# A hybrid encoder layer on one core: retention's products with the state split into high and low parts, divisions moved to ScalarE

## The reference, cut to what matters

```python
def sink_attention(q, k, v, valid, sinks):
    ...
    m = jnp.maximum(jnp.max(s, axis=-1, keepdims=True), sink)
    p = jnp.exp(s - m)
    w = p / (jnp.sum(p, axis=-1, keepdims=True) + jnp.exp(sink - m))
    return jnp.einsum('...hgqk,...khd->...qhgd', w.astype(v.dtype), v)

def retention_block(state, q, k, v, log_g):
    ...
    s = jnp.einsum('blhd,bmhd->bhlm', q, k) * decay
    intra = jnp.einsum('bhlm,bmhe->blhe', s, v)
    cross = jnp.einsum('blhd,bhde->blhe', q, state) * jnp.exp(log_g[None, :] * (n[:, None] + 1.0))[None, :, :, None]
    ...
    new_state = (jnp.exp(log_g * float(L))[None, :, None, None] * state
                 + jnp.einsum('blhd,blhe,lh->bhde', k, v, k_dec))
    return new_state, intra + cross
```

## Time and profile before

| | us |
|---|---|
| median of three runs (lowest, highest) | 969.23 (968.95, 969.66) |
| the profiled execution, its own time | 969.13 |
| span of that profile, first to last instruction | 967.30 |

### The profile page before, as it was taken

The page is one execution under the profiler, slowest core; times in us unless marked ns, Lnnn a source line. Parts: engine busy times, 40 slices in busy tenths (PEclk is TensorE's granted clock), DMA queues, the critical chain, the costliest instruction groups (busy, mean ns, idle before and its releaser), DMA issues.

```text
span 967.3 us, 19316 instructions
## 1 busy us (share of the span) xinstructions
PE 957.4 (99%) x7231; PEld 940.6 (97%) x7231; DVE 632.6 (65%) x1271; ACT 488.4 (50%) x955; POOL 158.4 (16%) x222
## 2 busy tenths in 40 slices
PE   8999999999999999999999999999999999999998
PEld 8999999999999999999999999999999999999998
DVE  5554776768666634345449677788778977755772
ACT  5333544445244522222546467776767767644352
POOL 2123212212110000000001202223222322230000
PEclk9999999999999999999999999999999999999999
DMA  8534221221222222344702537758876887776321
GB/s 218 151 114 136 65 70 50 71 77 50 78 71 64 79 77 81 95 121 142 218 23 61 220 113 166 174 130 176 185 171 136 177 184 161 169 225 198 88 56 44
DMA packets 178026, 118.12 MB, mean 122 GB/s; under 512 B 16224, under 2 KB 167168, under 8 KB 177680
## 3 DMA queue, kind: packets, MB, share of 16 engines
q1 hardware_dynamic: 160192, 79.19, 28.9%
q0 software_dynamic: 15856, 36.07, 17.6%
q10 hardware_dynamic: 1888, 1.64, 0.6%
HBM read 86.79 MB, written 10.75 MB: 101 GB/s over the span
## 4 chain that ended last, share of the span: by engine, by line
PE 94%; DVE 3%; issue 1%; ACT 1%; DMA 0%; POOL 0%; SPq 0%; DVEq 0%; POOLq 0%; ACTq 0%
PE acc L799 35%; PE acc L1081 13%; PE acc L1082 13%; PE acc L1083 13%; PE small L1081 4%; PE small L1083 4%; PE small L1082 4%; PE small L945 1%; PE small L962 1%; PE small L998 1%; PE acc L907 1%; PE small L1259 1%; DVE wlo L1872 0%; PE small L954 0%; DMA x_row<-in_x_sample 0%
## 5 line engine op out<-in xcount | busy, mean ns | idle before, releaser
L799 PE MATMUL acc<-xh,whi 128*128 128x288 f32 x720 | 158.7, 301 | 2.9 <-DVE wlo L1872 2.5
L799 PE MATMUL acc<-xl,whi 128*128 128x288 f32 x720 | 153.4, 294 | 0.0
L799 PE MATMUL acc<-xh,wlo 128*128 128x288 f32 x720 | 153.4, 294 | 0.0
L1291 ACT ACTIVATE whi<-raw 128x1024 fp32r<-128x1024 f32 (+1 forms) x60 | 60.1, 1001 | 130.0 <-PE acc L799 128.4
L799 PEld LDWEIGHTS acc<-xh,whi 128*128 128x128 f32 x720 | 113.9, 188 | 9.1 <-issue 7.7
L799 PEld LDWEIGHTS acc<-xh,wlo 128*128 128x128 f32 x720 | 115.0, 188 | 0.0
L799 PEld LDWEIGHTS acc<-xl,whi 128*128 128x128 f32 x720 | 114.9, 188 | 0.0
L1081 PE MATMUL acc<-yh,whi 128*128 128x288 f32 x380 | 112.9, 297 | 0.0
L1083 PE MATMUL acc<-yh,wlo 128*128 128x288 f32 x380 | 112.0, 295 | 0.0
L2800 POOL DMA_DIRECT2D wlo<-raw x80 | 69.0, 863 | 240.6 <-ACT wlo L1540 235.5
L1872 DVE TENSOR_TENSOR wlo<-raw,whi 128x1024 fp32r<-128x1024 f32 (+1 forms) x62 | 71.7, 1156 | 44.1 <-ACT whi L1291 43.4
(11 more groups left out here) (391 smaller groups left out, 2497.3 us busy)
## 6 DMA issues: line engine op xcount, KB each, us to landing
raw<-in_w_in SPq DMA_DIRECT2D x91, 256.0 KB, 3.2
wlo<-raw POOLq DMA_DIRECT2D x56, 256.0 KB, 4.1
raw<-in_w_ffn_gate SPq DMA_DIRECT2D x44, 256.0 KB, 3.4
raw<-in_w_ffn_up SPq DMA_DIRECT2D x44, 256.0 KB, 4.0
raw<-in_w_ffn_down SPq DMA_DIRECT2D x40, 192.0 KB, 3.1
res<-x_scratch POOLq DMA_DIRECT2D x16, 288.0 KB, 4.3
wlo<-raw POOLq DMA_DIRECT2D x24, 192.0 KB, 3.8
raw<-in_w_branch_ret SPq DMA_DIRECT2D x16, 256.0 KB, 3.0
```

Of the source, the lines that this page charges most:

```text
L799: ins = nc.tensor.matmul(acc[:, a, hf, 0:HALF], w[:, s, at:at + P], x(k)[:, hf * HALF:(hf + 1) * HALF], start=first and n == 0 and m == 0, ...
L1291: nc.scalar.activation(whi[:, s, 0:n], raw[:, s, 0:n], ACT.Copy).then_inc(hi_ready, 1)
```

## The change

- The product with the state is split like the others: `dec` has three parts (`q_dec`, `s_dec`, `k_dec`), `dec_hi` and `dec_lo` with it. ACT copies the state to `state_hi` (128x256) in step B of tiles 0 to 3, DVE makes `state_lo` in step L of tiles 1 to 4, and PE's plain f32 product becomes three `fp32r` ones. `state_hi` lies in the memory of `k_row`, so its first copy waits for the transfers from there.
- The probabilities are multiplied by the reciprocal on ACT, in four instructions of one head each with the reciprocal as a per-partition scale, at the same place N.
- The copies for the last block go ahead of the sigmoid of unit 5 of head 3.

```diff
-        q_dec = place("q_dec", [P, 2, P])
-        dec_hi = place("dec_hi", [P, 2, P], F32R)
-        dec = place("dec", [P, 2, P], at=cursor[0])
-        dec_lo = place("dec_lo", [P, 2, P], F32R)
-        s_dec, k_dec = dec[:, 0, :], dec[:, 1, :]
+        dec_hi = place("dec_hi", [P, 3, P], F32R)
+        dec = place("dec", [P, 3, P], at=cursor[0])
+        dec_lo = place("dec_lo", [P, 3, P], F32R)
+        q_dec, s_dec, k_dec = (dec[:, n, :] for n in range(3))
...
@@ PE, retention
                 elif piece == "B":
-                    pe.wait_ge(ret_low, n + 1)
-                    pe.wait_ge(ret_qd, n + 1 + CREDIT)
+                    pe.wait_ge(ret_low, (2 * RT - 1) * r + 2 * c + 1)
...
-                    split_product(ret_o, 0, v, True, c == 0)
+                    split_product(ret_o, 1, v, True, c == 0)
                     if c > 0:
-                        nc.tensor.matmul(ret_o, q_dec[:, c % 2, :], (state_s if c == RT - 1 else state_p)[:, :],
-                                         start=False, stop=True)
-                    split_product(ret_dl, 1, v, True, True).then_inc(ret_B, 1)
+                        split_product(ret_o, 0, (state_hi[:, :], state_lo[:, :]), False, True)
+                    split_product(ret_dl, 2, v, True, True).then_inc(ret_B, 1)
@@ ACT, attention
+                elif piece == "N":
+                    act.wait_ge(att_den, n + 1)
+                    for j in range(GROUP):
+                        ins = nc.scalar.activation(prob[0:nq, j, k0:k1], prob[0:nq, j, k0:k1], ACT.Copy,
+                                                   scale=den[0:nq, j:j + 1])
+                    ins.then_inc(att_prob, 1)
@@ ACT, retention
+                elif piece == "B" and c < RT - 1:
+                    act.wait_ge(ret_state, n + 1 + CREDIT)
+                    if c == 0 and r == 0:
+                        act.wait_ge(out_done, 16 * 6)
+                    if c == RT - 2:
+                        act.wait_ge(state_in_s, 16 * (r + 1))
+                    nc.scalar.activation(state_hi[:, :], (state_s if c == RT - 2 else state_p)[:, :], ACT.Copy
+                                         ).then_inc(ret_high, 1)
@@ ACT, heads
                     if t == 5:
                         v_high(1, h)
+                        if h == RH - 1:
+                            act.wait_ge(att_staged, RH + 1)
+                            act.wait_ge(ckt_ready, 1)
+                            act.wait_ge(cache_in, 32)
+                            nc.scalar.activation(k_st[:, 0:P], ckt[:, :], ACT.Copy)
+                            nc.scalar.activation(v_st[:, 0, :], cva[:, :], ACT.Copy).then_inc(cache_staged, 1)
                     head_job(t, h)
                     pieces(2 * t + 1, b, r, h)
...
-            act.wait_ge(att_staged, RH + 1)
-            act.wait_ge(ckt_ready, 1)
-            act.wait_ge(cache_in, 32)
-            nc.scalar.activation(k_st[:, 0:P], ckt[:, :], ACT.Copy)
-            nc.scalar.activation(v_st[:, 0, :], cva[:, :], ACT.Copy).then_inc(cache_staged, 1)
@@ DVE, attention
                     nc.vector.reciprocal(den[0:nq, :], den[0:nq, :]).then_inc(att_den, 1)
-                    dve.wait_ge(att_den, n + 1)
-                    width = k1 - k0
-                    shares = den[0:nq, :].rearrange("p (j o) -> p j o", o=1).to_broadcast([nq, GROUP, width])
-                    nc.vector.tensor_tensor(prob[0:nq, :, k0:k1], prob[0:nq, :, k0:k1], shares, ALU.mult
-                                            ).then_inc(att_prob, 1)
@@ DVE, retention
                 if piece == "A":
-                    dve.wait_ge(ret_B, n + 1 + CREDIT - earlier_use(c))
+                    dve.wait_ge(ret_B, n + CREDIT)
...
                 elif piece == "L":
-                    dve.wait_ge(ret_high, n + 1)
+                    if c > 0:
+                        dve.wait_ge(ret_high, (2 * RT - 1) * r + 2 * c)
+                        nc.vector.tensor_tensor(state_lo[:, :], (state_s if c == RT - 1 else state_p)[:, :],
+                                                state_hi[:, :].bitcast(F32), ALU.subtract).then_inc(ret_low, 1)
+                    dve.wait_ge(ret_high, (2 * RT - 1) * r + 2 * c + 1)
                     nc.vector.tensor_tensor(dec_lo[:, :, :], dec[:, :, :], dec_hi[:, :, :].bitcast(F32), ALU.subtract
                                             ).then_inc(ret_low, 1)
```

More of the change, by code:

```diff
@@ L428, in encoder_layer @@
         ck_row = place("ck_row", [P, P])
+        state_hi = place("state_hi", [P, RV], F32R, at=cursor[0])
         k_row = place("k_row", [P, 2, P])
@@ L459, in encoder_layer @@
         grstd = place("grstd", [P, 1])
+        state_lo = place("state_lo", [P, RV], F32R)
         split_at = (nc.sbuf_usable_end - 3 * slab) // 32 * 32
@@ L571, in encoder_layer @@
         x_saved_v = sem("x_saved_v")
-        ret_kst, ret_qd, ret_A, ret_sd, ret_kd = (
-            sem("ret_kst"), sem("ret_qd"), sem("ret_A"), sem("ret_sd"), sem("ret_kd"))
+        ret_kst, ret_A, ret_sd, ret_kd = (
+            sem("ret_kst"), sem("ret_A"), sem("ret_sd"), sem("ret_kd"))
         ret_B, ret_state, ret_mom, ret_grstd, ret_norm, ret_C, ret_gated = (
@@ L985, in ret_piece @@
                     pe.wait_ge(v_rows, 2 * r + 2)
-                    if c == RT - 1:
-                        pe.wait_ge(state_in_s, 16 * (r + 1))
                     v = (v_hi[slot][:, c, :], v_lo[:, slot, c, :])
@@ L2015, in ret_piece @@
                 if piece == "A":
-                    dve.wait_ge(ret_B, n + 1 + CREDIT - earlier_use(c))
+                    dve.wait_ge(ret_B, n + CREDIT)
                     q = qr[:, span(slot, 1), c * P:(c + 1) * P].rearrange("p a n -> p (a n)")
-                    nc.vector.tensor_tensor(q_dec[:, c % 2, :], q, tab[:, span(T_QD + P * r, P)], ALU.mult).then_inc(ret_qd, 1)
+                    nc.vector.tensor_tensor(q_dec, q, tab[:, span(T_QD + P * r, P)], ALU.mult)
                     dve.wait_ge(ret_A, n + 1 + CREDIT)
@@ L2651, in settled @@
                 pool.sem_inc(passed, 1)
-            for s_ in (ret_kst, ret_qd, ret_A, ret_sd, ret_kd, ret_B, ret_state, ret_grstd, ret_norm, ret_C,
+            for s_ in (ret_kst, ret_A, ret_sd, ret_kd, ret_B, ret_state, ret_grstd, ret_norm, ret_C,
                        ret_gated):
```

## The result

The changed kernel takes 974.30 us (median of five runs, 973.05 to 975.10) against 969.23 for the kernel before: a ratio of 1.0048 with an interval of 1.0037 to 1.0059. It is slower by 5.1 us; the forecast was 972.5, and its range ended at 974.2. The profiled execution took 975.10 us, the longest of the five, with a span of 973.3.

What follows compares the result with a forecast made beforehand. The prediction took TensorE (PE) as the bound, busy 957.4 of 967.3 us. Its terms, -1.3 - 0.35 + 1.38 + 3 x (-0.45 + 1.20 + 0.45) = +3.3 us on 969.23, gave 972.5, range 969.6 to 974.2.

Steps and rivals of the forecast that it cites:

- products with the state: Tiles 1 to 4 of four heads: three split products take PE 0.08 us less than one f32 product, -1.3 us.
- the last block's copies: Before the last block's scores: copies made before the sigmoid end PE's wait for `v_st`, -0.35 us.
- stall before unit 2: Heads 1 to 3: PE's 0.78 us wait for `wlo` shrinks as DVE's rotation starts earlier, -0.45 us a head.
- `o_norm` of tile 2: Place 5, heads 1 to 3: POOL's rotation delays `dec_lo`, so PE's transposes of `o_norm` start late, +1.20 us a head.
- divisions at place 7: Heads 1 to 3: ACT's four divisions end after PE wants the probabilities for its transposes, +0.45 us a head.
- divisions of the last block: Place 7 of the last block: ACT runs the gate's sigmoid first, so PE gets the divisions late, +1.38 us.
- Who goes next, POOL or `dec_lo`: Place 5, after `state_lo`: POOL's waiting rotation goes first and `dec_lo` follows it, making PE wait +1.20 us a head.
- DVE keeps its turn: Rival, 0.22: at place 5 `dec_lo` follows `state_lo` and POOL waits for both; +1.1 us, 970.3.
- Cheap divisions: Rival, 0.08: ACT's four divisions run at the plain copy's pace, 1.33 us; 968.7 to 970.9.
- More is late: Rival, 0.10: before unit 2 the rotation's `tb` isn't earlier, because ACT's swaps slip further; +1.35 us on top, 973.9.
- It does what it seems to be for: Rival, 0.08: PE gets its probabilities in time everywhere, with fast divisions and POOL last; faster, 966.2 us.

Runs made afterwards that it cites:

- split_only: Changed kernel with only the products with the state split; divisions stay on VectorE, the last block's copies behind the sigmoid: 972.41 us, 1.0037.
- pool_later: Changed kernel, with GpSimd's rotation of unit 2 in heads 1 to 3 also waiting for tile 2's low part: 970.55 us, 1.0012.
- swaps_first: The kernel called reordered, with ACT's two rotation swaps of unit 0 also put ahead of its `split_hi`: 965.67 us, 0.9962.
- reordered: Changed kernel: `state_lo` of tiles 2 to 4 a place earlier, N first at place 7, last block's divisions ahead of the sigmoid: 966.40 us, 0.9978.

## Why the prediction was right and wrong

The direction and the mechanism of each part were right; the sum lacked one term that lay outside the edited third. By starts of PE's rows, after against before, each against the row ahead of it:

| term of the sum | forecast | measured |
|---|---|---|
| products with the state, 16 | -1.3 | -1.3 (16 x 0.08) |
| the last block's copies | -0.35 | -0.42 |
| stall before unit 2, three heads | -1.35 | -0.39, -0.41, -0.40: -1.20 |
| `o_norm` of tile 2, three heads | +3.60 | +1.21, +1.57, +1.35: +4.13 |
| divisions at place 7, three heads | +1.35 | +0.38, +0.38, +0.38: +1.14 |
| the row behind each of these six stalls | none | 6 x 0.06: +0.34 |
| divisions of the last block | +1.38 | +1.28 |
| to the merge | +3.3 | +4.0 |
| behind the merge | 0 | +1.95 in the profiled execution, none in some others |

- **Products**: step B of tile 1 went from 1.13 to 232.69 - 231.64 = 1.05 us, as forecast. PE's busy time doesn't show it: in the stretch it is 314.95 before and 314.99 after. Where PE stops, the tail of its last matmuls counts as busy; at 247.99 the row's idle time is 1.19, and the start moved by 1.35. Seven new stalls hide the 1.3 us.
- **Who goes next, POOL or `dec_lo`**: the step that decided the sign was right. It rested on one hand-over in head 0; split_only gives 1.21 in each head against the forecast 1.20, and pool_later takes it away. The page "SBUF — State Buffer" of the Trainium skill, section "Who interferes with whom", has the exclusion but not who follows: here the one that waits goes between two queued instructions of the other, in each of the three heads, here and in split_only. The rival "DVE keeps its turn" falls.
- **`o_norm`, mis-sized**: in two heads it is 0.36 and 0.14 later than in split_only, so only with the divisions there too. In h = 2, DVE's `moments` wait 0.50 us behind `stats`; in h = 3, POOL's power takes 0.69 instead of 0.54 us. Both stand at the same instruction in every profile that has the products and the divisions, whatever the order, and in no other, so they are not chance; why is open.
- **Divisions**: priced at 1.74 from the Exp with a per-partition bias; 1.72 measured. "Cheap divisions" falls. The last block's came behind the sigmoid, 1.28 late against 1.38.
- **Stall before unit 2**: 0.78 to 0.38, forecast 0.3; what is left is DVE waiting for ACT's swaps, shown by swaps_first. The rival "More is late" falls with it: its 973.9 is close to the measured time, but `tb` did come earlier.
- **"It does what it seems to be for"** was priced 966.2 and ruled out for want of fast divisions and of POOL going last. By order alone POOL goes last, and the divisions, as slow as forecast, still come in time: reordered takes 966.4.
- **The missing term**: I took everything behind the merge as unchanged because no line of it is edited. In part of the executions an accumulating transfer lands late there. Shown: in all three profiles with the wait, the instruction fetch lies inside the transfer and takes about 2 us, and in the eleven others it doesn't begin inside it; with 196 instructions more on PE the wait and the spread go, twice. That the change brings the fetch there by making PE's program 28 rows longer is argued: four kernels with the same rows were profiled without the wait. Not shown: what decides in a given execution whether the fetch falls there, and where the lengthened kernel before loses its time. The term is about 1 us of the median (5.1 us over the kernel before, 4.1 with the 196 more); without it the time, 973.24, lies inside the range.

## What to carry to other kernels

Price a new instruction on DVE by what it lets in: behind it, a waiting POOL instruction of 1.5 us goes first, so make the extra one where POOL is idle, as `state_lo` a place earlier. Of a moved division, look at what stands ahead of it in its new engine's order; here a sigmoid and two low parts turned a gain of 2.9 us into a loss of 4.0, and three moves in the order gave it back. And a change of PE's program length can move its instruction fetches against all later transfers: before 1 or 2 us are put down to an edit, run the kernel with its program padded.

## What the runs showed of the hardware that I had not expected

- One fetch of PE's instructions (16 KB) took 0.9 to 1.5 us of one transfer engine where it began as the 192 KB transfer ended and 1.8 to 2.1 inside it, and the transfer that it met landed 5.5 to 6.2 us behind its issue instead of 3.9 to 4.5.
- The same program's fetch began at 748.4 us in one execution and at 752.7 in another, while PE's and POOL's rows agree within 0.1 us.
- 196 increments of a semaphore among PE's matmuls cost next to nothing: 322.27 us against 322.28, and 313.71 against 313.50.
